# Row-wise roots, squares taken early, and a scaled and transposed output in a two-block fp32 transformer kernel

## The reference, cut to what matters

```python
x = x + 0.5 * swiglu(rmsnorm(x, g_ffn1), w1_gate, w1_up, w1_down)        # ffn1
p = rmsnorm(x, g_mix) @ w_in                  # heads, index heads, two latents cq and ckv
x = x + concat(sparse_attention(...), mla_attention(rmsnorm(cq), rmsnorm(ckv), ...)) @ w_out   # wo
x = x + 0.5 * swiglu(rmsnorm(x, g_ffn2), ...)                            # ffn2
x = rmsnorm(x, g_final)                                                  # end of block one
cx = cx + 0.5 * mc[2] * swiglu_2(modulate(rms_norm(cx, norm1_g), ...))   # ffn3, context part
x  = x  + 0.5 * ml[2] * swiglu_2(modulate(rms_norm(x, norm1_g), ...))    # ffn3
hx, hc = modulate(rms_norm(x, norm2_g), ...), modulate(rms_norm(cx, norm2_g), ...)
x = x + ml[5] * merge_branches(conv, attention(hx, hc), gates) @ w_out   # conv, bg, gc, ga, q, k, v, ba, wo2
x = x + 0.5 * ml[8] * swiglu_2(modulate(rms_norm(x, norm3_g), ...))      # ffn4
return rms_norm(x, final_g)
```

## Time and profile before

| | |
|---|---|
| median of three runs | 2885.19 us (2883.59 to 2889.8) |
| the profiled execution, its own time | 2889.41 us |
| its span, first to last instruction | 2887.4 us |
| busy: PE, DVE, ACT, POOL | 2744.3, 1455.1, 787.6, 320.4 us |
| mean granted TensorE clock | 0.964 |

### The profile page before, as it was taken

How to read it: one execution, slowest core, us unless ns; L and a number is a source line. 1 busy time by engine, 2 the same in 40 slices (tenths; PEclk the granted TensorE clock), 3 DMA queues, 4 the chain that set the end, 5 groups by cost and what they waited for, 6 DMA issues and landing times.

```text
span 2887.4 us, 34488 instructions
## 1 busy us (share of the span) xinstructions
PE 2744.3 (95%) x12448; PEld 2153.6 (75%) x12448; DVE 1455.1 (50%) x2510; ACT 787.6 (27%) x1040; POOL 320.4 (11%) x243
## 2 busy tenths in 40 slices
PE   7999999888888999998999999999999999999998
PEld 5888877634447888876888888878888657788886
DVE  6778786556647756565222222255325653433334
ACT  3121122234543312124211111132232352322212
POOL 0101020000001101010211301100200003110111
PEclk9999999959789999999999999999999999999999
DMA  4454443200024445441222221223332002233331
GB/s 134 138 142 135 132 135 81 54 15 1 1 66 115 130 141 150 134 124 30 62 69 59 60 71 55 62 59 101 90 108 73 30 1 73 73 102 88 102 85 61
DMA packets 394758, 241.03 MB, mean 83 GB/s; under 512 B 14768, under 2 KB 392752, under 8 KB 394672
## 3 DMA queue, kind: packets, MB, share of 16 engines
q1 hardware_dynamic: 394672, 239.92, 28.5%
HBM read 237.79 MB, written 2.10 MB: 83 GB/s over the span
## 4 chain that ended last, share of the span: by engine, by line
PE 87%; DVE 6%; ACT 4%; issue 1%; POOL 1%; DMA 1%; SPq 0%; DVEq 0%; ACTq 0%; POOLq 0%
PE PS L568 22%; PE PS L571 22%; PE PS L569 22%; PE PS L554 3%; PE PS L557 3%; PE PS L555 3%; PE PS L532 2%; PE PS L924 2%; PE PS L684 1%; PE PS L904 1%; DVE VA L1200 1%; DVE RB L1184 1%; POOL VA L1645 1%; PE PS L750 1%; PE PS L770 1%
## 5 line engine op out<-in xcount | busy, mean ns | idle before, releaser
L568 PE MATMUL PS<-NH,WH 128*128 128x512 f32 x2160 | 815.1, 377 | 26.7 <-DVE NL L1190 11.5
L569 PE MATMUL PS<-NL,WH 128*128 128x512 f32 x2160 | 792.6, 374 | 0.0
L571 PE MATMUL PS<-NH,WL 128*128 128x512 f32 x2160 | 751.7, 375 | 0.0
L951 ACT ACTIVATE WH<-RAW 128x2048 fp32r<-128x2048 f32 x190 | 363.7, 1914 | 576.5 <-PE PS L571 535.2
L1179 DVE TENSOR_TENSOR WL<-RAW,WH 128x2048 fp32r<-128x2048 f32 x190 | 461.7, 2430 | 114.0 <-ACT WH L951 113.6
L568 PEld LDWEIGHTS PS<-NH,WH 128*128 128x128 f32 x2160 | 408.5, 189 | 121.1 <-issue 28.8
L569 PEld LDWEIGHTS PS<-NL,WH 128*128 128x128 f32 x2160 | 408.5, 189 | 70.5
L571 PEld LDWEIGHTS PS<-NH,WL 128*128 128x128 f32 x2160 | 384.7, 190 | 58.0
L568 PE MATMUL PS<-HH,WH 128*128 128x512 f32 x880 | 329.4, 374 | 1.4 <-DVE WL L1179 1.3
L1219 DVE SCALAR_TENSOR_TENSOR RB<-MW,CV,RB 128x128 f32<-128x128 f32 x826 | 319.8, 419 | 17.8
L569 PE MATMUL PS<-HL,WH 128*128 128x512 f32 x880 | 320.1, 373 | 0.0
(11 more groups left out here) (234 smaller groups left out, 2602.3 us busy)
## 6 DMA issues: line engine op xcount, KB each, us to landing
RAW<-in_ffn_w_in SPq DMA_DIRECT2D x88, 512.0 KB, 4.6
MW<-in_w_mod SPq DMA_DIRECT2D x72, 512.0 KB, 3.8
RAW<-in_w_in SPq DMA_DIRECT2D x70, 512.0 KB, 4.4
RAW<-in_w_gate SPq DMA_DIRECT2D x44, 512.0 KB, 4.3
RAW<-in_w_up SPq DMA_DIRECT2D x44, 512.0 KB, 5.5
RAW<-in_w_down SPq DMA_DIRECT2D x32, 512.0 KB, 4.7
RAW<-in_ffn_w_out SPq DMA_DIRECT2D x32, 512.0 KB, 4.0
RAW<-in_w_out SPq DMA_DIRECT2D x16, 512.0 KB, 4.4
```

The costliest lines, as they stand in the source:

```text
L568: pe.matmul(o, wh, xh(k), start=k == 0, stop=False)
L569: pe.matmul(o, wh, xl(k), start=False, stop=False)
L571: last = pe.matmul(o, wl, xh(k), start=False, stop=k == kn - 1)
L951: act.activation(WH[1 - s][:, :], RAW[1 - s][:, :], ACT.Copy).then_inc(w_hi, 1)
```

## The change: what it does

1. **Roots for each token, in a column.** Squares become the stationary operand, four products of one column each (two for the context) give the sums as `[128 tokens, 1]` columns; ACT's root and DVE's reciprocal work on 128x4. DVE then scales the unit matrix by each column (`diagonal`, in `RB`), and the PE spreads the roots over the partitions with ones times diagonal, 128x128 for each of the four. The scaling of `X` reads the spread roots from PSUM (`norm_bank`).
2. **Squares taken early.** In the last `down` of each layer ACT squares the tiles as they come free (`split_and_square`); POOL adds 1 to 6, so that the PE sums two products. In the last block (`TAILS`) the PE makes one half after the other, and `half_mm`, `half_x` let tile 6 go ahead of tile 7.
3. **Split ahead.** ACT makes `WH` of the stage's second block ahead of `norm_high`.
4. **Order in `tiles`/`tile` with a norm.** The PE waits for the high part alone, makes the products of both halves with it, then waits for the low part. Order of `tiles` everywhere: wh0 xh, wh1 xh, wl0 xh, wl1 xh, wh0 xl, wh1 xl. `VA` has three slots for 512 tokens; POOL makes the low parts 3, 5 and 7 in norms of eight tiles without a shift.
5. **Idle products:** 4 ahead of the spread and 5 behind it in place of 24 ahead.
6. **norm_c2** moves into the bg stage, its sums behind bg's first block, its spread behind the second.
7. **Start.** ACT squares and sums each token tile along its row as it lands; transposes are copied four at a time. The first block's weights are split in two halves (POOL makes the second `WL` half), the two first `MW` DMAs go behind the second block's weights.
8. **End.** `X` times gain is transposed in the last stage (`out_scaled`, `out_turned`), copied into `OUTB` by ACT (`out_copied`), and scaled there by each token's root; four DMAs follow.
9. **Layout.** `RT` (32 bytes) is declared ahead of `HH`; `CX` stands between `HH` and `HL`. `HH` then begins at 148,352, `HL` at 181,120, `YH` and `MH` at 181,120, `YL` and `ML` at 197,504, all multiples of 64.

```diff
+        RT = sb("RT", [P, 2 * NT])
         ff = ExitStack()
         HH = sb("HH", [P, HMAX, T + TC], F32R, ff)
+        CX = sb("CX", [P, KD, TC], F32, ff)
         HL = sb("HL", [P, HMAX, T + TC], F32R, ff)
-        CX = sb("CX", [P, KD, TC], F32, ff)
...
+            def norm_sums(m, banks_free):
+                sums = (0, m.n - 1) if m.early else range(m.n)
...
+                    for t in range(m.cols):
+                        last = pe.matmul(norm_bank(m)[:, t:t + 1], squares(m, k)[:, t * P:(t + 1) * P], ones[:, 0:1],
+                                         start=i == 0 and t == 0, stop=k == m.n - 1, skip_group_check=True)
+            def norm_spread(m, banks_free):
                 wait(pe, psum_free, banks_free)
-                if m.dst and m.tok == T and m.n == KD:
-                    busy(WARM)
+                warm_up = m.dst and m.tok == T and m.n == KD
+                if warm_up:
+                    busy(4)
+                for t in range(m.cols):
+                    pe.wait_ge(norm_dg, m.dg + t + 1)
+                    pe.matmul(norm_bank(m)[:, t * P:(t + 1) * P], ones[:, :], diagonal(m, t), start=True, stop=True)\
+                        .then_inc(norm_bc, 1)
+                if warm_up:
+                    busy(5)
...
+                    w = [wt(half, k) for half in range(2)]
+                    for x, (xh, xl) in enumerate(xs):
+                        for half in range(2):
+                            pe.matmul(outs[half][x], w[half][0], xh(k), start=k == 0, stop=False)
+                        for half in range(2):
+                            pe.matmul(outs[half][x], w[half][1], xh(k), start=False, stop=False)
+                    if m is not None:
+                        pe.wait_ge(*low_ready(m, k))
+                    for x, (xh, xl) in enumerate(xs):
+                        for half in range(2):
+                            last = pe.matmul(outs[half][x], w[half][0], xl(k), start=False, stop=k == kn - 1)
...
+                    if isinstance(b, int) and b in TAILS:
+                        tile(banks[0][s], lambda k: wt(0, k), xs, kn, ready).then_inc(half_mm, 1)
+                        if b == NB - 1:
+                            out_turned(KD - 4)
+                            out_turned(KD - 3)
+                        last = tile(banks[1][s], lambda k: wt(1, k), xs, kn)
...
+            for n in range(KD // 2):
+                pairs(bg_b + n, 1, XS, xb, KD, straight=True)
+                if n == 0:
+                    norm_sums(norm_c2, None)
+                elif n == 1:
+                    norm_spread(norm_c2, None)
...
+            def norm(m, ahead=None):
+                norm_roots(m, KD - 2 if m.early else 0)
+                if ahead is not None:
+                    split(ahead % 2, loaded(ahead, 1), ahead)
                 norm_high(m)
...
+            for t in range(NT):
+                act.wait_ge(x_loaded[t], 16)
+                act.activation(XSQ[:, t, :], XIN[:, t, :], ACT.Square, accum_out=RT[:, t:t + 1]).then_inc(x_sq, 1)
...
+            def norm_inverse(m):
                 dve.wait_ge(norm_rms, m.no + 1)
                 own.settle(dve, dve.reciprocal(roots(m), roots(m)))
+                for t in range(m.cols):
+                    dve.tensor_scalar(diagonal(m, t), ident[:, :], roots(m)[:, t:t + 1], None, ALU.mult)\
+                        .then_inc(norm_dg, 1)
...
+            for t in (0, 2, 3):
+                ins = dve.tensor_scalar(OUTB[:, t, :], OUTB[:, t, :], RT[:, t:t + 1], None, ALU.mult)
+                ins.then_inc(out_ready[t], 1)
...
+            def lows(m):
+                for k in m.pooled:
+                    pool.wait_ge(norm_hi, m.low + k + 1)
+                    h, l = m.dst(k)
+                    pool.tensor_tensor(l, scaled(m, k), h.bitcast(F32), ALU.subtract).then_inc(norm_lo2, 1)
```

More of the change, by code:

```diff
@@ L261, in __init__ @@
                 self.ready = ready
-                self.base, self.no = sum(m.n for m in norms), len(norms)
-                self.early, self.sums = early, 3 if early else n
-                self.mm, self.acc = sum(m.sums for m in norms), sum(m.n - 3 for m in norms if m.early)
+                self.base, self.no = sum(m.n for m in norms if m.applied), sum(not m.rows for m in norms)
+                self.rows, self.sq = rows, sum(m.n for m in norms if not m.rows)
+                self.applied = True
@@ L266, in __init__ @@
+                self.early, self.sums = early, 0 if rows else 2 if early else n
+                self.pooled = (3, 5, 7) if dst and not shift and n == KD else ()
+                self.lo, self.lo2 = sum(m.n - len(m.pooled) for m in norms if m.dst), sum(len(m.pooled) for m in norms)
+                self.mm, self.acc = sum(m.sums for m in norms), sum(m.n - 2 for m in norms if m.early)
                 self.low = sum(m.n for m in norms if m.dst)
+                self.cols = tok // P
+                self.dg = sum(m.cols for m in norms)
@@ L273, in squares, with norm_bank @@
+        def norm_bank(m):
+            return B[4] if m is norm_c1 else B[5] if m in (norm_c2, norm_kv, norm_x1) else B[7]
         def squares(m, k):
+            if m.tok < T:
+                return SA[:, k % 2, T:T + TC]
             return VA[:, 0, 0:m.tok] if m.early and k == 0 else SA[:, k % 2, 0:m.tok]
@@ L630, in _ @@
             pe.wait_ge(c2_s, 2)
-            transposes(lambda t: XIN[:, t // KD, (t % KD) * P:(t % KD + 1) * P], 0, x_loaded)
-            norm(norm1, None)
+            for t in range(NT):
+                x_turned(t)
+                if t:
+                    x_spread(t - 1)
+            x_spread(NT - 1)
+            busy(8)
             ffn(ffn1, norm1, H0["ffn1"], XS, HS, xb, m0=M0["ffn1"])
@@ L862, in _ @@
                     if b == k_b:
-                        last = tile([KXB[half], KCB[half]], wt, XCS, KD, (norm_lo, norm_c2.low))
+                        last = tile([KXB[half], KCB[half]], wt, XCS, KD, (norm_lo, norm_c2.lo))
                     else:
@@ L999, in _ @@
[L999 to L1001 removed]
+                    if j == 0:
+                        act.activation(warm[:, :], eps[:, :], ACT.Sqrt)
+                    else:
+                        norm_squares(m, 2 * j - 2, 2 * j)
+                    if m is norm_out and j > 1:
+                        for k in range(2 * j - 4, 2 * j - 2):
+                            out_copied(k)
@@ L1091, in _ @@
             norm_roots(norm_x1)
+            b = ffn3[0][0]
+            split(b % 2, loaded(b, 1), b)
             norm_high(norm_c1)
             norm_high(norm_x1)
-            ffn(ffn3, T + TC)
-            norm_roots(norm_x2)
-            norm_roots(norm_c2)
-            norm_high(norm_x2)
-            gate_up(conv_b, KD, T, func=ACT.Copy)
+            ffn(ffn3, T + TC, norm_x2)
+            norm(norm_x2, conv_b)
+            gate_up(conv_b, KD, T, func=ACT.Copy, ahead=True)
             for b, j, s, at in stage(act, bg_b, KD // 2, True):
```

352 lines of the change are left out of this document (245 added, 107 removed).

## The result

The changed kernel takes **2822.22 us** (median of four runs, 2816.79 to 2824.82) for 2885.01 (2883.59 to 2889.8): the ratio is 0.9777, its 95% interval 0.9761 to 0.9793. It is faster by 62.8 us. The profiled execution took 2822.73 us with a span of 2820.9, 66.5 less than the span before; its mean granted clock is 0.959 for 0.964.

A forecast was written before the change was run, and what follows sets the result against it. The PE was taken to bound the kernel, its pace inside stages and its waits at norms, start and end. Eight terms summed to 68.2 us, giving 2818 us for the median, +-13 (2805 to 2832), with 2796 to 2838 at about 0.8.

The forecast's parts named there:

- rival (a): Matmuls with HH, YH, MH moving: starts at multiples of 64 bytes speed the PE, 13.1 us more, 2805 us; chance 0.27.
- Start: Kernel start to the second block, which waits for DVE: begins at 33.0 against 52.10, gain 19 us (14 to 22).
- ffn1 to w_in: Between these stages: ACT's moved split waits for late weights, landing near timeline point 433; gain 3 us (1 to 6).
- wo to ffn2: Between these stages, to the second block: shorter chain, POOL's low parts relieve DVE; gain 6.3 us (4 to 9).
- wo2 to ffn4: Between these stages, to the second block: shorter norm chain and split ahead; gain 7.5 us.
- ffn2 to ffn3: Between these stages, through norm_c1 and norm_x1: first matmul at 1322.3 for 1329.95, gain 7.7 us (5 to 12).
- norm_q and norm_kv: At the latents: shorter reciprocals, and sums falling to under 1 us for norm_kv; gain 7.5 us (4 to 9).
- ffn3 to conv: Between these stages: chain 13.1 us shorter, norm_c2's sums come back in bg; net gain 9 us (6 to 12).
- The end: Behind the last main matmul: landing 11 us earlier, less 2.7 for transposes in the stage; net 8.2 us (5 to 11).
- (b): Rival, first blocks behind norms: the removed idle products are missed, 3.4 us each in five places, 2835 us; chance 0.11.
- (c): Rival at the norms: ACT's order eats the chain, half of the middle terms are lost, 2843 us; chance 0.09.
- (d): Rival in tiles: changing PSUM bank at each of 9312 matmuls costs 124 us, 2942 us, slower; chance 0.03.

The follow-up runs named there:

- e4: The changed kernel with two idle 128x128 products behind each of the 16 column sums of norm_c1 and norm_x1: 2821.73 us.
- e5: The changed kernel with one high part of norm_c1 behind each square of norm_x1 in ACT's order: 2809.34 us.
- e2: The changed kernel with 32 unused bytes ahead of HH, so HH, YH and MH begin 32 past a multiple of 64: 2834.59 us.
- e12: The changed kernel with 32 bytes ahead of RAW and 32 behind WL, so the weights begin 32 bytes past a multiple of 64: 2863.31 us.
- e8: The changed kernel with the idle products of the kernel before, 24 ahead of the spread and none behind: 2835.07 us.
- e9: The changed kernel with norm_kv's two squares ahead of norm_q's high parts in ACT's order, norm_kv's root behind them: 2815.68 us.
- e7: The kernel before with only the changed kernel's order of products in tiles: 2879.04 us.
- e10: The kernel of e5 with norm_x1's squares added up by POOL, so that the PE sums two products: 2812.46 us.
- e3: The changed kernel with the order of products of before in tiles wherever no norm is awaited: 2825.75 us.
- e11: The changed kernel with e5, e9 and POOL adding up norm_c2's squares, all three together: 2802.04 us.
- e1: The kernel before with 32 unused bytes ahead of HH, so HH, HL, YH, YL, MH and ML begin at multiples of 64: 2866.25 us.

## Why the prediction was right, and where it was wrong

2822.2 for 2818 said, inside 2796 to 2838. That the change is faster by the norms, the start and the end is right. That the sum came out so near is luck: three terms fell short by 22.6 us (15.8, 3.5 and 3.3), and what the forecast had at nothing or too low brought 22.3 (11.4 in other stages, most of it the layout, 6.4 in ffn3, 4.5 at the end). The forecast and rival (a), which I set against each other, are both true.

- **Start, ffn1 to w_in, wo to ffn2, wo2 to ffn4: right**, within 1.2 us each. At w_in the wait that I had named, ACT's moved split for SP's late weights, is in the trace: at 411.22 it has waited 2.08 us for the DMA, 11.0 us behind ffn1's last main matmul, for the 11.5 of my 433.
- **ffn2 to ffn3: wrong by 15.8 us.** The step that failed is "ACT squares norm_x1's tiles (eight of 0.63, until 1309.9)". Counted from ffn2's last main matmul, I had norm_c1's squares begin after 10.1 us, its sums end after 14.5, norm_x1's after 20.6, norm_c1 ready after 30.0, the first matmul after 33.0. The trace has 13.6, 19.7, 35.2, 44.3 and 48.7. So 9.4 of the 15.8 are norm_x1's sums. I priced ACT and took the PE's four products, 0.6 us by my price, to fit beside it; they took 1.71, of which 0.82 would be left at the full clock (e4). 5.2 us are ahead of them (the context's transposes and norm_c1's sums), 1.1 in what follows. "Splits ahead (1.9) and only then rounds c1" was seen, but as a fixed cost. e5 shows that this order alone costs 8.0 us: without it the stretch is 40.75 us, for the 40.64 before. Nor did I ask what the column form costs where eight squares are summed: in the kernel before, the same sums of norm_x1 had 512 columns and the full clock, and took 7.68 us for 13.65. No run puts the wide form back there.
- **norm_q and norm_kv: the mechanism right, the term mis-sized**, 4.0 for 7.5. Norm_kv's 16 records take 3.58 us, "under 1" in my text: 0.213 us each, the lower clock again. The same sums at 512 columns took 3.37, so the column form saves nothing there.
- **ffn3 to conv: the terms mis-sized, 5.7 for 9.** The chain gave 10.7 for 13.1. The sums in bg cost 5.0 (a gap of 5.25 for one of 0.23), where I had 3.6 (bounds 2 and 6): 32 records of 0.112 us, 3.6 us, and hand-overs on top. That conv's second block agrees is right: it begins 13.02 us behind the first in both kernels. Before, the first block went at the norm's pace; now it is through earlier and the second waits 1.9 us for its `WL`, which DVE splits only behind the norm and a memset.
- **The end: better than said.** From the start of the last main matmul to the end of the span it is 11.8 us for 24.5.
- **Rival (a): true**, 13.1 said, 12.4 in e2. (By its own figures 2.80 over 2.72 is 1/34 more and not 1/32; no run tests a mechanism in pieces of 64 bytes.) I held it at 0.27 since NH and HH had one pace in ffn3. e12 says why that evidence was weak: in ffn3 starts hardly show at all. **(b)** refuted by e8. **(c)** is true in kind, ACT's order eating the chain, at ffn2 to ffn3 (e5) and at the latents (e9), though by squares and high parts in the queue and not by late weights or a table load. **(d)** refuted by e7.
- **The lock between DVE and GpSimd** (the Trainium skill, SBUF — State Buffer, section "SBUF: two separate sides") was the rule by which the sum would be 3 us lower. The trace of e10 agrees with the lock: DVE's low parts, with two SBUF inputs, took 0.98 us beside POOL's additions for 0.48. But the 3 us are not there. POOL makes low parts at the start, at w_in and at ffn2 (not at ffn4, whose norm has a shift). Each took 1.27 to 1.33 us and began 0.1 us behind ACT's rounding; DVE's own kept to 0.7. At ffn2 one modulation product took 1.31 us beside the last of them, for 0.28. wo to ffn2 came in 0.7 us under the forecast, the start 0.3 over it.

What stays open: the second attention took 147.8 us in seven of the profiles (before, after, e3, e4, e5, e10, e11) and 144.5 to 144.9 in the other seven, with no edit in it; wo took 48.6 us in the kernel before and 45.3 to 46.4 in all thirteen others, e1 and e7 among them, whose wo is that of before. Other stages come in two lengths some 1.6 us apart, edit or none: ffn1 at 367.4 or 369.0, w_in at 66.8 or 68.4. No run separates a cause, and one profile's length of a stage carries it.

## What to carry to other kernels

Between two stages, price each engine's part at the clock that it will have there, the PE's small products too, and look for the queue that two neighbouring chains share: the sum of a square in four columns cost 1.7 us there, and two changes of ACT's order gave back 8.0 and 4.2 us. Mechanisms that don't exclude each other are added, not weighed as rivals. And look at the starts of both matmul operands: 32 bytes decided over 12 us (e2) and 41 us (e12) here.

## What the runs showed of the hardware

- Moving 512 columns of fp32r, the PE issues one matmul in 226.7 ns when both operands begin at multiples of 64 bytes, and in 233.3 ns when either the moving (e2) or the stationary one (e12) begins 32 bytes past one. With both past one no run was made. The weight load lies beside the matmul ahead of it, and still its start counts.
- A one-column f32 product with 128 columns to load is two records, one every 0.112 us at 2.4 GHz and every 0.213 at 1.2: a sum of four columns was 0.82 us (e4) or 1.7 us. In 34 us of such products, idle products and a wait of 7.7 us the granted clock stayed at 0.50.
- DVE's reciprocal of 128x4 took 0.17 us, that of 128x512 3.35.
- DVE scaled 128x1024 by a column, with its one tensor input in SBUF, in 0.7 us; the scaling of 128x512 with a second tensor input in PSUM took 0.74 (changed kernel).
- DVE's low part of 128x256 took 0.98 us beside a POOL addition and 0.48 without, POOL's addition 1.27 us beside it (e10).
